# High and low parts of the weights of a transformer step: two tiles against one interleaved tile

## The chip, the cores and the metric

One core of one Trainium2 chip runs the whole program in one launch. The metric is the device time of one execution in microseconds (us); lower is better.

## The reference, cut to what matters

A sequence of 256 tokens with 1,024 channels goes through two blocks. The first has a feed-forward block, a mixer ("pool") and a second feed-forward block, each behind a norm that is modulated by nine vectors made from a condition `c`. The second has two attention mixers ("window" and "causal") and a last norm.

```python
def swiglu(n, w_gate, w_up, w_down):
    return (jax.nn.silu(n @ w_gate) * (n @ w_up)) @ w_down     # 1024 x 2816, 1024 x 2816, 2816 x 1024

mod = (jax.nn.silu(c) @ w_ada[l] + b_ada[l])[:, None, :]
h = h + 0.5 * gt1 * swiglu(modulate(rmsnorm(h, g_ffn1[l]), sh1, sc1), ...)
h = h + gt2 * hybrid_mixer(modulate(rmsnorm(h, g_mix[l]), sh2, sc2), ...)
h = h + 0.5 * gt3 * swiglu(modulate(rmsnorm(h, g_ffn2[l]), sh3, sc3), ...)
...
for i in range(2):                      # window attention, then block attention with all past blocks
    q, k, v, z = split_proj(rmsnorm_2(h, norm_g[i]), w_in, n_kv)
    o = attention(q, k, v).reshape(B, S, MIX_WIDTH) * jax.nn.silu(z)
    h = h + o @ w_out[i]
```

Everything is float32. The products with weight matrices are nearly all of the work.

## The kernel before

The weights stream in as 105 units of 1 MB: 128 partitions of 2,048 elements (`UNIT`). A gate, up or input unit is 8 chunks of 128 rows by 256 columns; a down unit is 2 chunks by 1,024 columns. There are three slots (`NS`), and unit `u` uses slot `u % 3`. SyncE loads a unit into `raw` as soon as the low part of the unit three before it has been made.

A float32 product is made of three passes in the type float32r. ScalarE writes the rounded high part of a unit (`high`, L620, `whi<-raw`), VectorE the rest (`low`, L948, `wlo<-raw,whi`; `low_half` L956 does it in two halves at the end of the pool mixer). The activations are split in the same way (`nhi`/`nlo`, `hhi`/`hlo`, `yhi`/`ylo`). TensorE then forms three matmuls into one accumulator for each 128 x 128 tile of weights and 256 tokens (`split_product`, L1416 to L1418):

```python
mm(to, stat_hi, mov_hi, ...)     # L1416
mm(to, stat_hi, mov_lo, ...)     # L1417
mm(to, stat_lo, mov_hi, ...)     # L1418
```

In each of them the weights are the stationary operand: a weights load (LDWEIGHTS, shown on PEld) reads 128 elements of each partition, and the matmul then streams 256 moving columns. A unit is 16 tiles, so 48 loads and 48 matmuls. The two feed-forward blocks have 33 units each, 1,584 matmuls; the mixers have 39 units. `project` does gate, up and input units; `project_two` two units at once at the start of a block; `down` (in `ffn`) the down units, and `out_product` the output matrices of the first two mixers.

In three places the weights move and the activations stand still: `project_rows` (L1522 to L1524) for the value units V and half of the unit KV, and `out_rows` (L1721 to L1723) for the four output units of the last mixer, with 512 moving columns.

The order of all work is written out by hand: each engine runs its own program, a loop of 9 turns for most of a feed-forward block and a list of steps (`mixer_plan`) for the mixers. In the built program every partition has `whi` at byte 41,088, `wlo` at 65,664, `nhi` at 123,200 and `nlo` at 131,392; `hhi`, `hlo`, `yhi` and `ylo` start, like `nhi`, at 320 modulo 1,024, and the weight tiles at 128 modulo 512. A load walks 512 bytes of a partition, a matmul with 256 moving columns 1,024.

The tile names in the profile are out<-moving,stationary: `sc<-nhi,wlo` is a matmul into bank `sc` with moving `nhi` and stationary `wlo`.

Of the kernel before, what the change touches and what calls it, by code (L numbers as in the profile page):

```python
# [24 lines left out]
P = 128  # L25
# [138 lines left out]

BY_ROWS = range(28, 36)

CHAINED = range(8, 28)
# [33 lines left out]
def build(nc, x, c, w_ada, b_ada, g_ffn1, w1_gate, w1_up, w1_down, g_mix, w_in, w_pool, pool_scale, w_out,  # L203
          g_ffn2, w2_gate, w2_up, w2_down, g_final, norm_g_2, w_in_a_2, sinks_a_2, w_in_b_2, w_out_2,
          final_g_2, shape_consts, out):
    with ExitStack() as ctx:
        def sb(name, shape, dt=F32):
            return ctx.enter_context(nc.sbuf_tensor(name, shape, dt))
# [3 lines left out]


        raw = sb("raw", [P, NS, UNIT])
        whi = sb("whi", [P, NS, UNIT], F32R)
        wlo = sb("wlo", [P, NS, UNIT], F32R)
        ada = sb("ada", [P, 2, DC, UC])
        macc = sb("macc", [P, 2, UC])
        hT = sb("hT", [P, DC, S])
# [177 lines left out]
        block = ctx.enter_context(nc.Block())  # L397


        def rows8(t, s):  # L400
            return t[:, s, :].rearrange("p (c n) -> p c n", c=DC)

        def rows2(t, s):
            return t[:, s, :].rearrange("p (c n) -> p c n", c=2)

        def by_chunk(w):
            return w.rearrange("(c p) n -> p c n", p=P)
# [205 lines left out]
        def _(act):  # L613
            def high(u, reps=None, by=None):

                if u >= UNITS:
                    return
                n = 16 * (u // NS + 1)
                act.wait_ge(landed[u % NS], n + 16 * reps if reps is not None else n)
                nc.scalar.activation(whi[:, u % NS], raw[:, u % NS], ACT.Copy).then_inc(hi_done, 1)  # L620

            def squares(k, chunks=range(DC)):
                for m in chunks:
# [310 lines left out]
        def _(dve):  # L934
# [8 lines left out]
            def low(u, reps=None):  # L943

                if u >= UNITS:
                    return
                dve.wait_ge(hi_done, u + 1 + (3 * reps if reps is not None else 0))
                nc.vector.tensor_tensor(wlo[:, u % NS], raw[:, u % NS], whi[:, u % NS].bitcast(F32),  # L948
                                        ALU.subtract).then_inc(lo_done, 1)

            def low_half(u, i):

                if i == 0:
                    dve.wait_ge(hi_done, u + 1)
                at = slice(i * UNIT // 2, (i + 1) * UNIT // 2)
                ins = nc.vector.tensor_tensor(wlo[:, u % NS, at], raw[:, u % NS, at], whi[:, u % NS, at].bitcast(F32),  # L956
                                              ALU.subtract)
                if i:
                    ins.then_inc(lo_done, 1)

# [450 lines left out]
        def _(pe):  # L1411
# [75 lines left out]
                pe.wait_ge(macc_done, q + 1)  # L1487
                select_sums(q, start_ps[q])

            def project(bank, slot, k=None, chunks=(0, 1), over=range(DC)):  # L1490

                hi, lo = rows8(whi, slot), rows8(wlo, slot)
                order = [(m, ch) for m in chunks for ch in range(DC)]
                if k is not None:
                    order = [(m, ch) for ch in over for m in chunks]
                for m, ch in order:
                    if k is not None and m == 0:
                        pe.wait_ge(nlo_done, DC * tnum[k] + ch + 1)
                    at = slice(m * P, (m + 1) * P)

                    ins = split_product(bank[:, m * S:(m + 1) * S], hi[:, ch, at], lo[:, ch, at],
                                        nhi[:, ch], nlo[:, ch], ch == 0 and (k is None or m == 0), ch == DC - 1)
                return ins

            def project_two(banks, slots, k, signals):

                for step in range(DC + 2):
                    for n, ch in ((0, step), (1, step - 2)):
                        if 0 <= ch < DC:
                            ins = project(banks[n], slots[n], k, over=range(ch, ch + 1))  # L1510
                            if ch == DC - 1:
                                ins.then_inc(signals, 1)

            def project_rows(bank, slot, col, width, at0):

                hi, lo = rows8(whi, slot), rows8(wlo, slot)
                for b in range(2):
                    for ch in range(DC):
                        tok = slice(b * P, (b + 1) * P)
                        to = bank[:, at0 + b * width:at0 + (b + 1) * width]  # L1520
                        w = slice(col, col + width)
                        mm(to, nhi[:, ch, tok], hi[:, ch, w], start=(ch == 0), stop=False, skip_group_check=True)  # L1522
                        mm(to, nhi[:, ch, tok], lo[:, ch, w], start=False, stop=False, skip_group_check=True)
                        ins = mm(to, nlo[:, ch, tok], hi[:, ch, w], start=False, stop=(ch == DC - 1),  # L1524
                                 skip_group_check=True)
                return ins

            def job(st):
# [23 lines left out]
                if kind == "U":  # L1552
                    if st["i"] == 0:
                        pe.wait_ge(lo_done, u + 2)
                        project_two((acc[p % 2], acc[(p + 1) % 2]), (u % NS, (u + 1) % NS), MIX_NORM["pool"], job_done)
                    return
                pe.wait_ge(lo_done, u + 1)
                k = MIX_NORM[st["mixer"]] if st["first"] else None
# [2 lines left out]
                if kind == "V":  # L1561
                    if st["rcol"]:
                        token_columns(MIX_NORM[st["mixer"]])
                    ins = project_rows(bank, u % NS, 0, UC, 0)
                elif kind == "KV":
                    project(bank, u % NS, k, chunks=(0,))
                    ins = project_rows(bank, u % NS, P, P, S)
                elif st["rcol"]:
                    project(bank, u % NS, chunks=(0,))
                    token_columns(MIX_NORM[st["mixer"]])  # L1570
                    ins = project(bank, u % NS, chunks=(1,))
                elif kind == "Q" and st["next"]["kind"] == "TPV":
                    project(bank, u % NS, chunks=(0,))
                    if st["mixer"] == "pool":
                        pe.wait_ge(mod_done, 32)
                    transposes(st["next"], 0)
                    transposes(st["next"], 1)
                    ins = project(bank, u % NS, chunks=(1,))
                elif kind == "Z":
                    project(bank, u % NS, chunks=(0,))  # L1580
                    scores(st["next"], (0, 1))
                    ins = project(bank, u % NS, chunks=(1,))
                else:
                    ins = project(bank, u % NS, k)
                ins.then_inc(job_done, 1)
                if st["first"] and st["mixer"] != "pool":
                    sum_squares(STAT[k], None, True, True)
# [111 lines left out]

            def out_product(st, j, m, chunks, first, last):  # L1700

                hi, lo = rows8(whi, st["u"] % NS), rows8(wlo, st["u"] % NS)
                at = slice(m * P, (m + 1) * P)
                for ch in chunks:
                    if j == 0 and m == 0:
                        y_ready(st, ch)
                    to = out_acc[RESIDUAL[MIX_NORM[st["mixer"]] + 1]][j]
                    ins = split_product(to[:, m * S:(m + 1) * S], hi[:, ch, at], lo[:, ch, at], yhi[:, ch],
                                        ylo[:, ch], first and ch == chunks[0], last and ch == chunks[-1])
                return ins  # L1710

            def out_rows(u, j, chunks):

                tok = slice(j % 2 * P, (j % 2 + 1) * P)
                to = out_acc["last"][j][:, :]
                for ch in chunks:
                    if j == 0:
                        y_ready(PLANS["causal"][-1], ch)
                    slot, i = (u + ch // 4) % NS, ch % 4
                    hi, lo = [t[:, slot, :].rearrange("p (c n) -> p c n", c=4)[:, i] for t in (whi, wlo)]  # L1720
                    mm(to, yhi[:, ch, tok], hi, start=False, stop=False, skip_group_check=True)  # L1721
                    mm(to, yhi[:, ch, tok], lo, start=False, stop=False, skip_group_check=True)  # L1722
                    ins = mm(to, ylo[:, ch, tok], hi, start=False, stop=ch == DC - 1, skip_group_check=True)  # L1723
                return ins
# [99 lines left out]
            def ffn(f):  # L1824
                base, n0, k = FFN_UNIT[f], FB * f, FFN_NORM[f]

                def gate(u, i, reps=None, norm=None):
                    add = reps if reps is not None else 0
                    pe.wait_ge(lo_done, u + 1 + 3 * add)
                    if n0 + i > 0:  # L1830
                        pe.wait_ge(silu_done, n0 + i + add)
                    project(sc[0], u % NS, norm).then_inc(ffn_used, 1)

                def up(u, i, reps=None):
                    add = reps if reps is not None else 0
                    pe.wait_ge(lo_done, u + 1 + 3 * add)
                    if n0 + i > 0:
                        pe.wait_ge(hid_done, n0 + i + add)
                    project(sc[1], u % NS).then_inc(ffn_used, 1)

                def down(u, i, reps=None, buf=0):
                    add = reps if reps is not None else 0
                    hi, lo = rows2(whi, u % NS), rows2(wlo, u % NS)
                    first = reps is None and i == 0
                    pe.wait_ge(lo_done, u + 1 + 3 * add)
                    pe.wait_ge(hlo_done, n0 + i + 1 + add)
# [11 lines left out]
                else:  # L1858
                    pe.wait_ge(lo_done, base + 2)
                    pe.wait_ge(silu_done, n0)  # L1860
                    pe.wait_ge(hid_done, n0)
                    project_two(sc, (base % NS, (base + 1) % NS), k, ffn_used)
                gate(base + 2, 1)
                up(base + 3, 1)
                for m, ins in down(base + 4, 0):
# [110 lines left out]
```

## Time and profile before

| what | us |
|---|---|
| median of 3 executions (lowest, highest) | 743.36 (743.33, 750.12) |
| the profiled execution | 743.8 |
| its span, first to last instruction | 742.0 |
| TensorE matmul busy in it | 710.3 |

The profile is one execution. Starts are counted from the span's start. PE is TensorE's matmuls, PEld its weights loads, DVE VectorE, ACT ScalarE, POOL GpSimd. Matmuls overlap one another, so the distance between two starts, not the length of one, says how fast TensorE goes; a stretch's length divided by the number of matmuls in it gives the same.

### The profile page before, as it was taken

The numbers are of one execution on the slowest core, as the hardware profiler recorded it, in microseconds if no ns is written. First come the engines' busy times: TensorE is split into PE (matmuls) and PEld (weight loads), VectorE is DVE, ScalarE is ACT, GpSimd is POOL, SyncE is SP. The second block draws the span as 40 slices with busy tenths as digits, with TensorE's granted clock in tenths as the row PEclk, the third lists the DMA queues.
The fourth block names the chain that finished last, engine by engine and source line by source line (L and its number), as shares of the span: only waits on it lengthen the run. The fifth ranks groups of instructions, "written<-read, shape, count | busy, mean of one in ns | idle before, by whom it ended". The sixth has DMA issues, their size and how long they took to land.

```text
span 742.0 us, 14116 instructions
## 1 busy us (share of the span) xinstructions
PE 710.3 (96%) x5888; PEld 661.4 (89%) x5888; DVE 489.8 (66%) x738; ACT 367.1 (49%) x559; POOL 77.1 (10%) x73
## 2 busy tenths in 40 slices
PE   5599999999999999989999999999999999999997
PEld 4299999999998988869999999999888889888875
DVE  2469789877866446566445544555989986787853
ACT  4154344343454346546343334336676666746652
POOL 0000066000010680000000000000600002000000
PEclk9589999999998999999999999999999999999999
DMA  9999999998956753275556556555333344554301
GB/s 337 382 362 303 331 372 325 350 327 319 345 180 226 269 193 110 84 229 164 178 179 203 183 174 200 191 170 170 114 115 115 116 147 135 170 163 123 114 1 57
DMA packets 102100, 152.59 MB, mean 206 GB/s; under 512 B 2600, under 2 KB 84268, under 8 KB 101932
## 3 DMA queue, kind: packets, MB, share of 16 engines
q1 hardware_dynamic: 101828, 151.75, 60.2%
q8 instruction: 28, 0.46, 0.3%
q10 hardware_dynamic: 232, 0.28, 0.1%
q14 instruction: 12, 0.10, 0.0%
HBM read 150.97 MB, written 1.05 MB: 205 GB/s over the span
## 4 chain that ended last, share of the span: by engine, by line
PE 42%; DVE 8%; ACT 5%; issue 1%; ACTq 0%; DVEq 0%
PE sc L1416 6%; PE sc L1417 6%; PE sc L1418 6%; PE acc L1416 5%; PE acc L1417 5%; PE acc L1418 5%; DVE wlo L948 3%; ACT whi L620 2%; PE acc L1721 1%; PE acc L1723 1%; PE acc L1722 1%; ACT nhi L649 1%; PE sc L1609 1%; DVE vp L1134 1%; ACT vp L747 1%
## 5 line engine op out<-in xcount | busy, mean ns | idle before, releaser
L948 DVE TENSOR_TENSOR wlo<-raw,whi 128x2048 fp32r<-128x2048 f32 x104 | 241.2, 2321 | 114.8 <-ACT whi L620 114.6
L620 ACT ACTIVATE whi<-raw 128x2048 fp32r<-128x2048 f32 x105 | 200.1, 1908 | 67.5 <-PE sc L1418 59.6
L1416 PE MATMUL sc<-nhi,whi 128*128 128x256 f32 x704 | 197.7, 281 | 2.0 <-DVE nlo L1386 1.6
L1417 PE MATMUL sc<-nlo,whi 128*128 128x256 f32 x704 | 197.2, 280 | 0.0
L1418 PE MATMUL sc<-nhi,wlo 128*128 128x256 f32 x704 | 197.2, 280 | 0.0
L1416 PEld LDWEIGHTS sc<-nhi,whi 128*128 128x128 f32 x704 | 134.9, 192 | 2.5 <-issue 2.5
L1417 PEld LDWEIGHTS sc<-nlo,whi 128*128 128x128 f32 x704 | 133.4, 190 | 0.0
L1418 PEld LDWEIGHTS sc<-nhi,wlo 128*128 128x128 f32 x704 | 133.3, 189 | 0.0
L1416 PE MATMUL acc<-nhi,whi 128*128 128x256 f32 x376 | 109.4, 291 | 2.9 <-DVE wlo L948 1.7
L1417 PE MATMUL acc<-nlo,whi 128*128 128x256 f32 x376 | 104.5, 278 | 0.0
L1418 PE MATMUL acc<-nhi,wlo 128*128 128x256 f32 x376 | 104.4, 278 | 0.0
L1417 PE MATMUL acc<-hlo,whi 128*128 128x256 f32 x320 | 89.1, 279 | 0.0
L1416 PE MATMUL acc<-hhi,whi 128*128 128x256 f32 x320 | 89.1, 279 | 0.0
L1418 PE MATMUL acc<-hhi,wlo 128*128 128x256 f32 x320 | 89.1, 279 | 0.0
L1416 PEld LDWEIGHTS acc<-nhi,whi 128*128 128x128 f32 x376 | 70.8, 188 | 12.0 <-issue 7.6
L1417 PEld LDWEIGHTS acc<-nlo,whi 128*128 128x128 f32 x376 | 70.9, 189 | 0.5 <-issue 0.5
L1418 PEld LDWEIGHTS acc<-nhi,wlo 128*128 128x128 f32 x376 | 70.8, 188 | 0.0
L1416 PEld LDWEIGHTS acc<-hhi,whi 128*128 128x128 f32 x320 | 60.8, 190 | 0.0
L1417 PEld LDWEIGHTS acc<-hlo,whi 128*128 128x128 f32 x320 | 60.1, 188 | 0.0
L1418 PEld LDWEIGHTS acc<-hhi,wlo 128*128 128x128 f32 x320 | 60.1, 188 | 0.0
L1416 PE MATMUL acc<-yhi,whi 128*128 128x256 f32 x160 | 46.8, 292 | 2.0 <-DVE hT L972 1.4
L555 POOL TENSOR_TENSOR std<-sq 128x256 f32<-128x256 f32 x4 | 2.9, 736 | 411.4 <-DVE nlo L1005 200.9
(248 smaller groups left out, 1084.7 us busy)
## 6 DMA issues: line engine op xcount, KB each, us to landing
ada<-in_w_ada_dram SPq DMA_DIRECT2D x23, 1024.0 KB, 7.6
raw<-in_w_gate_dram SPq DMA_DIRECT2D x22, 1024.0 KB, 5.4
raw<-in_w_up_dram SPq DMA_DIRECT2D x22, 1024.0 KB, 5.9
raw<-in_w_down_dram SPq DMA_DIRECT2D x22, 1024.0 KB, 4.9
raw<-in_w_out_dram SPq DMA_DIRECT2D x12, 1024.0 KB, 5.0
raw<-in_w_in_b_dram SPq DMA_DIRECT2D x10, 1024.0 KB, 5.2
xo<-in_w_ada_dram SPq DMA_DIRECT2D x9, 1024.0 KB, 7.5
raw<-in_w_in_a_dram SPq DMA_DIRECT2D x9, 1024.0 KB, 5.2
```

The lines of the kernel that those rows point to most:

```text
L620: nc.scalar.activation(whi[:, u % NS], raw[:, u % NS], ACT.Copy).then_inc(hi_done, 1)
L649: nc.scalar.activation(nhi[:, m], hT[:, m], ACT.Copy, scale=input_gain(k, m)).then_inc(nhi_done, 1)
L747: ins = nc.scalar.activation(prob[:, s, lo:up], prob[:, s, lo:up], ACT.Exp, scale=-1.0, bias=nm[:, s, b:b + 1], accum_out=den[:, s, b:b + 1])
L948: nc.vector.tensor_tensor(wlo[:, u % NS], raw[:, u % NS], whi[:, u % NS].bitcast(F32), ALU.subtract).then_inc(lo_done, 1)
L1134: ins = nc.vector.tensor_tensor_reduce(out=prob[:, s, lo:up], in0=sc[h % 2][:, lo:up], in1=mask[:, lo:up], scale=-1.0, scalar=largest, op0 ...
L1416: mm(to, stat_hi, mov_hi, start=first, stop=False, skip_group_check=True)
L1417: mm(to, stat_hi, mov_lo, start=False, stop=False, skip_group_check=True)
L1418: return mm(to, stat_lo, mov_hi, start=False, stop=last, skip_group_check=True)
L1609: mm(rot_ps[:, :], rotation, src[:, :, :].rearrange("p b n -> p (b n)"), start=True, stop=True).then_inc(rot_done, 1)
L1721: mm(to, yhi[:, ch, tok], hi, start=False, stop=False, skip_group_check=True)
L1722: mm(to, yhi[:, ch, tok], lo, start=False, stop=False, skip_group_check=True)
L1723: ins = mm(to, ylo[:, ch, tok], hi, start=False, stop=ch == DC - 1, skip_group_check=True)
```

## The change

`whi` and `wlo` (two tiles of 3 x 2,048) become one tile `wpair` of 3 x 4,096 at the same place, and everything else keeps its address. In 97 of the 105 units element n of the high part lies at place 2n and element n of the low part at 2n + 1. There ScalarE writes with a step of 8 bytes, VectorE reads the high part and writes the low part with a step of 8 bytes, and a weights load reads 128 elements with a step of 8 bytes, 1,024 bytes from first to last, starting at 128 or 132 modulo 1,024. The 8 units in `APART` (three V, one KV, the last four output units) keep both halves apart, each contiguous. No instruction is added, removed or moved on any engine; `parts` and `rows` replace `rows8` and `rows2`, and functions take the unit's number instead of its slot.

```diff
+APART = [st["u"] for steps in PLANS.values() for st in steps if st["kind"] in ("V", "KV")]
+APART += range(UNITS - 4, UNITS)
...
-        whi = sb("whi", [P, NS, UNIT], F32R)
-        wlo = sb("wlo", [P, NS, UNIT], F32R)
+        wpair = sb("wpair", [P, NS, 2 * UNIT], F32R)
...
-        def rows8(t, s):
-            return t[:, s, :].rearrange("p (c n) -> p c n", c=DC)
-
-        def rows2(t, s):
-            return t[:, s, :].rearrange("p (c n) -> p c n", c=2)
+        def parts(u):
+            both = wpair[:, u % NS, :]
+            if u in APART:
+                return both[:, 0:UNIT], both[:, UNIT:2 * UNIT]
+            return [both.rearrange("p (n t) -> p n t", t=2)[:, :, t] for t in range(2)]
+
+        def rows(u, chunks):
+            return [t.rearrange("p (c n) -> p c n", c=chunks) for t in parts(u)]
...
-                nc.scalar.activation(whi[:, u % NS], raw[:, u % NS], ACT.Copy).then_inc(hi_done, 1)
+                nc.scalar.activation(parts(u)[0], raw[:, u % NS], ACT.Copy).then_inc(hi_done, 1)
...
-                nc.vector.tensor_tensor(wlo[:, u % NS], raw[:, u % NS], whi[:, u % NS].bitcast(F32),
-                                        ALU.subtract).then_inc(lo_done, 1)
+                hi, lo = parts(u)
+                nc.vector.tensor_tensor(lo, raw[:, u % NS], hi.bitcast(F32), ALU.subtract).then_inc(lo_done, 1)
...
-            def project(bank, slot, k=None, chunks=(0, 1), over=range(DC)):
-
-                hi, lo = rows8(whi, slot), rows8(wlo, slot)
+            def project(bank, u, k=None, chunks=(0, 1), over=range(DC)):
+
+                hi, lo = rows(u, DC)
...
-                hi, lo = rows8(whi, st["u"] % NS), rows8(wlo, st["u"] % NS)
+                hi, lo = rows(st["u"], DC)
...
-                    slot, i = (u + ch // 4) % NS, ch % 4
-                    hi, lo = [t[:, slot, :].rearrange("p (c n) -> p c n", c=4)[:, i] for t in (whi, wlo)]
+                    hi, lo = [t[:, ch % 4] for t in rows(u + ch // 4, 4)]
...
-                    hi, lo = rows2(whi, u % NS), rows2(wlo, u % NS)
+                    hi, lo = rows(u, 2)
```

## Rows read from the trace of the kernel before

**Rows 1.** Page: busy time by engine; busy tenths of 40 slices.

```profile
span 742.0 us, 14116 instructions
...
PE 710.3 (96%) x5888; PEld 661.4 (89%) x5888; DVE 489.8 (66%) x738; ACT 367.1 (49%) x559; POOL 77.1 (10%) x73
...
PE   5599999999999999989999999999999999999997
...
PEclk9589999999998999999999999999999999999999
```

**Rows 2.** Waits of TensorE, longest first.

```profile
PE sc L1902 <- DMA kd<-in_b_ada_dram: 7.7, 1, 7.7
...
PE acc L1416 <- DVE wlo L948: 1.7, 1, 1.7
```

**Rows 3.** Windows: half-clock start, both feed-forward blocks, the last two mixers.

```profile
core 0: us, PE busy (x) PEld busy (x) DVE busy (x) ACT busy (x) POOL busy (x), PEclk, DMA share, GB/s
37.08:42.28 5.20, 5.20 (x26) 5.20 (x26) 3.93 (x7) 5.20 (x7) 0.00 (x0) 0.50 1.06 395
42.85:213.42 170.57, 170.57 (x1507) 170.57 (x1506) 138.18 (x95) 70.61 (x53) 24.57 (x12) 1.00 0.95 336
332.85:512.11 179.26, 179.26 (x1523) 179.26 (x1523) 91.43 (x63) 75.82 (x60) 0.00 (x0) 1.00 0.57 183
521.00:707.00 186.00, 181.19 (x1473) 159.72 (x1474) 153.76 (x356) 121.77 (x270) 15.79 (x19) 1.00 0.41 131
```

**Rows 4.** Timeline (start, length), first feed-forward block: two starts three matmuls apart.

```profile
...
149.95 0.28 PE L1416 MATMUL sc<-nhi,whi 128*128 128x256 f32 x1
...
150.29 0.28 PE L1416 MATMUL sc<-nhi,whi 128*128 128x256 f32 x1
...
```

**Rows 5.** Timeline, second feed-forward block: three matmuls apart.

```profile
...
399.87 0.28 PE L1416 MATMUL sc<-nhi,whi 128*128 128x256 f32 x1
...
400.22 0.28 PE L1416 MATMUL sc<-nhi,whi 128*128 128x256 f32 x1
...
```

**Rows 6.** Line L1416, 60 to 200 us: durations min/median/max ns.

```profile
L1416 PE MATMUL acc<-hhi,whi x144: 276/276/276, 61.2 to 196.9; 128*128 128x256 f32 x144
L1416 PEld LDWEIGHTS acc<-hhi,whi x144: 187/188/188, 61.1 to 196.8; 128*128 128x128 f32 x144
```

**Rows 7.** Line L1416, 345 to 505 us.

```profile
L1416 PE MATMUL acc<-hhi,whi x144: 281/281/282, 353.9 to 494.9; 128*128 128x256 f32 x144
L1416 PEld LDWEIGHTS acc<-hhi,whi x144: 192/192/192, 353.8 to 494.8; 128*128 128x128 f32 x144
```

**Rows 8.** Timeline at half clock: three matmuls apart.

```profile
...
40.07 0.41 PE L1416 MATMUL sc<-nhi,whi 128*128 128x256 f32 x1
...
40.71 0.41 PE L1416 MATMUL sc<-nhi,whi 128*128 128x256 f32 x1
...
```

**Rows 9.** Timeline, matmuls with 128 moving columns: first and last of 18.

```profile
...
527.77 0.27 PE L1522 MATMUL acc<-whi,nhi 128*128 128x128 f32 x1
...
529.66 0.28 PE L1524 MATMUL acc<-whi,nlo 128*128 128x128 f32 x1
...
```

**Rows 10.** Groups of matmuls, 215 to 331 us.

```profile
L1418 PE MATMUL acc<-nhi,wlo 128*128 128x256 f32 x96 | 26.8, 279 | 0.0
...
L1418 PE MATMUL acc<-yhi,wlo 128*128 128x256 f32 x80 | 22.3, 279 | 0.0
```

**Rows 11.** Groups of matmuls, 513 to 722 us.

```profile
L1418 PE MATMUL acc<-nhi,wlo 128*128 128x256 f32 x280 | 77.6, 277 | 0.0
...
L1417 PE MATMUL acc<-ylo,whi 128*128 128x256 f32 x80 | 22.3, 279 | 0.0
```

**Rows 12.** Line L948 on VectorE, 43 to 213 us, and L620 on ScalarE, whole span.

```profile
L948 DVE TENSOR_TENSOR wlo<-raw,whi x32: 2278/2293/3095, 42.8 to 211.6; 128x2048 fp32r<-128x2048 f32 x32
...
L620 ACT ACTIVATE whi<-raw x105: 1888/1907/1924, 20.1 to 721.7; 128x2048 fp32r<-128x2048 f32 x105
```

**Rows 13.** Page: the chain that ended last, by engine and line.

```profile
PE sc L1416 6%; PE sc L1417 6%; PE sc L1418 6%; PE acc L1416 5%; PE acc L1417 5%; PE acc L1418 5%; DVE wlo L948 3%; ACT whi L620 2%; PE acc L1721 1%; PE acc L1723 1%; PE acc L1722 1%; ACT nhi L649 1%; PE sc L1609 1%; DVE vp L1134 1%; ACT vp L747 1%
```

More of the change, by code:

```diff
@@ L955, in low_half @@
                 at = slice(i * UNIT // 2, (i + 1) * UNIT // 2)
-                ins = nc.vector.tensor_tensor(wlo[:, u % NS, at], raw[:, u % NS, at], whi[:, u % NS, at].bitcast(F32),
-                                              ALU.subtract)
+                hi, lo = parts(u)
+                ins = nc.vector.tensor_tensor(lo[:, at], raw[:, u % NS, at], hi[:, at].bitcast(F32), ALU.subtract)
                 if i:
@@ L1503, in project, with project_two @@
                 return ins
-            def project_two(banks, slots, k, signals):
+            def project_two(banks, units, k, signals):
                 for step in range(DC + 2):
@@ L1509, in project_two, with project_rows @@
                         if 0 <= ch < DC:
-                            ins = project(banks[n], slots[n], k, over=range(ch, ch + 1))
+                            ins = project(banks[n], units[n], k, over=range(ch, ch + 1))
                             if ch == DC - 1:
                                 ins.then_inc(signals, 1)
-            def project_rows(bank, slot, col, width, at0):
-                hi, lo = rows8(whi, slot), rows8(wlo, slot)
+            def project_rows(bank, u, col, width, at0):
+                hi, lo = rows(u, DC)
                 for b in range(2):
@@ L1554, in job @@
                         pe.wait_ge(lo_done, u + 2)
-                        project_two((acc[p % 2], acc[(p + 1) % 2]), (u % NS, (u + 1) % NS), MIX_NORM["pool"], job_done)
+                        project_two((acc[p % 2], acc[(p + 1) % 2]), (u, u + 1), MIX_NORM["pool"], job_done)
                     return
@@ L1563, in job @@
                         token_columns(MIX_NORM[st["mixer"]])
-                    ins = project_rows(bank, u % NS, 0, UC, 0)
+                    ins = project_rows(bank, u, 0, UC, 0)
                 elif kind == "KV":
-                    project(bank, u % NS, k, chunks=(0,))
-                    ins = project_rows(bank, u % NS, P, P, S)
+                    project(bank, u, k, chunks=(0,))
+                    ins = project_rows(bank, u, P, P, S)
                 elif st["rcol"]:
-                    project(bank, u % NS, chunks=(0,))
+                    project(bank, u, chunks=(0,))
                     token_columns(MIX_NORM[st["mixer"]])
-                    ins = project(bank, u % NS, chunks=(1,))
+                    ins = project(bank, u, chunks=(1,))
                 elif kind == "Q" and st["next"]["kind"] == "TPV":
-                    project(bank, u % NS, chunks=(0,))
+                    project(bank, u, chunks=(0,))
                     if st["mixer"] == "pool":
@@ L1577, in job @@
                     transposes(st["next"], 1)
-                    ins = project(bank, u % NS, chunks=(1,))
+                    ins = project(bank, u, chunks=(1,))
                 elif kind == "Z":
-                    project(bank, u % NS, chunks=(0,))
+                    project(bank, u, chunks=(0,))
                     scores(st["next"], (0, 1))
-                    ins = project(bank, u % NS, chunks=(1,))
+                    ins = project(bank, u, chunks=(1,))
                 else:
-                    ins = project(bank, u % NS, k)
+                    ins = project(bank, u, k)
                 ins.then_inc(job_done, 1)
@@ L1831, in gate @@
                         pe.wait_ge(silu_done, n0 + i + add)
-                    project(sc[0], u % NS, norm).then_inc(ffn_used, 1)
+                    project(sc[0], u, norm).then_inc(ffn_used, 1)
                 def up(u, i, reps=None):
@@ L1838, in up @@
                         pe.wait_ge(hid_done, n0 + i + add)
-                    project(sc[1], u % NS).then_inc(ffn_used, 1)
+                    project(sc[1], u).then_inc(ffn_used, 1)
                 def down(u, i, reps=None, buf=0):
                     add = reps if reps is not None else 0
-                    hi, lo = rows2(whi, u % NS), rows2(wlo, u % NS)
+                    hi, lo = rows(u, 2)
                     first = reps is None and i == 0
@@ L1861, in ffn @@
                     pe.wait_ge(hid_done, n0)
-                    project_two(sc, (base % NS, (base + 1) % NS), k, ffn_used)
+                    project_two(sc, (base, base + 1), k, ffn_used)
                 gate(base + 2, 1)
```

## The prediction

> **What bounds the kernel now.** I read the page's first parts, then TensorE's waits, then windows and timelines of its long stretches. TensorE is busy in 710.3 of 742.0 us, at full clock in nearly every slice after the start [rows 1]. Its waits are small: the longest is 7.7 us at the start, the longest for a weight's low part 1.7 us [rows 2]. So the time is TensorE's own pace, 5,040 matmuls on weights (105 units of 48) and some 850 others.
>
> That pace is not one number. In the first feed-forward block 1,507 matmuls fill 170.57 us, 113.2 ns each; in the second 1,523 fill 179.26 us, 117.7 ns each [rows 3]. The timelines agree: three matmuls take 0.34 us in the one and 0.35 in the other [rows 4, 5]. Code, shapes, slots and addresses are the same, the granted clock is 1.00 in both, no wait stands in either, and the faster block has more traffic beside it (DMA share 0.95 against 0.57, VectorE 138 us against 91). I call the two paces the short step and the long step. They differ in one thing: in the long step the load of line L1416 takes 192 ns where it took 188, and a matmul 281 where it took 276 [rows 6, 7]. A block begins in one step and stays in it to its end.
>
> Two more rows set the floor. At half clock (0.50) a step is 0.64 us / 3 = 213 ns [rows 3, 8], so at full clock the same columns alone would need 107 ns, and the short step is 6 ns above that. With only 128 moving columns 17 steps take 1.89 us, 111 ns each [rows 9]: there the contiguous load, not the streaming, sets the step. So loads come within 2 ns of the short step, and anything that lengthens them by more shows in the total.
>
> The Trainium skill ("TensorE: Matmul & The Clock Gate", "LDWEIGHTS (loading the stationary operand)") gives a load as columns / 1.2 GHz whatever it reads; for 128 that is an estimate of 107 ns, and the 111 ns of [rows 9] agree. By it the load would be as long after the change as before, and the layout could act only by how load and streaming meet.
>
> **The change part by part.** No instruction comes, goes or moves. What changes is the step of addresses in 97 units.
>
> *TensorE.* Before, a load walks 512 bytes while the matmul beside it walks 1,024; afterwards both walk 1,024, so their distance in memory stays the same through a step, whichever tile it is. The long step looks like the two streams meeting: it appears with nothing else changed, is kept up by the rhythm of hi, hi, lo, and lengthens one load of the three. If equal walks remove the meeting, every step becomes the short one. I take 113.2 ns from the first block and count against the profiled execution:
> - second block: 1,584 x (117.7 - 113.2) = 7.1 us;
> - last down unit of the first block, 48 matmuls at 279 ns where the block had 276 (within [rows 10]): 0.2 us;
> - mixers: their 1,488 changed matmuls are at mean lengths of 277 to 279 ns against 276 [rows 10, 11]. Per line, 96 x 3 + 64 x 3 (the 80 less 16 of that down unit) early and 280 x 1 + 64 x 3 late, times three lines, is 2.9 us. TensorE is busy in 181 of 186 us there [rows 3], but VectorE and ScalarE also stand in the chain, so I let two thirds count: 1.9 us.
>
> Together 9.2 us. The profiled execution took 743.8 us (its span 742.0 and 1.8 around it), 0.4 above the median of 743.36, so I subtract there: 743.8 - 9.2 = 734.6 us.
>
> No row shows a load with a step of 8 bytes. From below it is bounded by the contiguous load, 111 ns [rows 9]; from above by the slowest pace of a step in the trace, 213 ns [rows 8]. I take the contiguous value, to which every full-clock row is near, and keep the rest for the range.
>
> *ScalarE and VectorE.* A high part is 1,907 ns and a low part 2,293 ns in the median [rows 12]. No row has a step of 8 bytes on a tile of this size either. From below I bound it at no change, as the element count, engine and type stay; from above at twice the length. I take no change. Cover: in the first feed-forward block VectorE is idle for 170.6 - 138.2 = 32.4 us, and holds 32 low parts there [rows 3, 12]; each could grow by 1.0 us, 44%, before VectorE sets the pace. In the mixers there is less: `wlo` is 3% and `whi` 2% of the chain [rows 13], 37 us, so a tenth more costs up to 3.7 us.
>
> The rule that speaks to this is the Trainium skill's on lines of 16 bytes ("Advanced Engine Details and Errata", "Memory Cachelines"): full rate needs at least two accesses in each line. A step of 8 bytes leaves exactly two fp32, so by the rule loads, reads and writes cost what they did and the sum stands; but nothing is to spare, and where two hits fall short the fourth rival holds. No row of this trace has such a step, so the rule is neither borne out nor refuted here.
>
> *SyncE, DMA, waits.* A unit is loaded when the low part three units before is done; unchanged. In the first block a step shorter than 113 ns would ask for more than the 336 GB/s of [rows 3]; the start shows 395, so there is room for the 2% of the first rival.
>
> **The rivals.**
> 1. *The short step shrinks too.* If its 6 ns above 107 also come from meeting, both blocks fall to the load's 111 ns: 1,536 x 2.0 = 3.1, 1,584 x 6.5 = 10.3, the last down unit 0.3, mixers 1,488 x 4.0 x 2/3 = 4.0 us, 17.7 in all: 726 us. For it: half clock shows no loss over the streaming. Against it: the 6 ns stay the same over 1,507 matmuls, whatever else runs; they look like the moving operand's own.
> 2. *Nothing changes.* If the step is chosen by where TensorE stood when a block began, the layout has no say: 743.4 us. For it: the same addresses gave both steps. Against it: one load in three is longer in the long step, so loads take part. Were load and streaming balanced at a step between the two, the first block's loss and the second's gain would cancel, and it would come to the same.
> 3. *The long step everywhere.* If equal walks make load and streaming meet always, the first block pays 1,536 x 4.5 = 6.9 us and the mixers 1,488 x 4.5 less the 2.9 they have, two thirds of it, 2.5: 753 us.
> 4. *The load becomes the bound* (slower). A load now passes through twice as many bytes. If it meets the streaming twice as often, the long step's extra doubles to 9 ns everywhere: 1,536 x 9 = 13.8, 1,584 x 4.5 = 7.1, mixers (1,488 x 9 - 2.9 us) x 2/3 = 7.0, so 772 us. Place: every load of the 97 units; it decides as soon as a load passes 113 ns, 2 above [rows 9]. At the upper bound of 213 ns it would be 3,168 x 98 ns = 310 us in the blocks and about 97 in the mixers, some 1,150 us. For it: the margin is only 2 ns. Against it: most of a load's 188 ns is already beside a matmul, and the long step prolongs one in three by only 4.
> 5. *Slower engines.* Twice 2,293 ns would put 73 us more on VectorE in the first block, 41 over its idle time, and up to 37 in the mixers: about 820 us.
>
> **How the numbers follow.** Forecast, short step everywhere: 0.36. Rival 1: 0.10, rival 2: 0.22, rival 3: 0.11, rival 4: 0.14, rival 5: 0.07. Faster by over 1%, which is about what a measurement here can tell from no change, means below 735.9 us. My 734.6 is barely under it: with mixers that give nothing it would be 736.5, with all of theirs 733.6; and 731 to 739 is its own range. So I give three quarters of it, 0.28, to faster and 0.08 to the same: faster 0.28 + 0.10 = 0.38; same 0.08 + 0.22 = 0.30; slower 0.11 + 0.14 + 0.07 = 0.32. The range 724 to 774 holds the forecast, rivals 1 to 3 and rival 4 at 772; what lies outside is rival 5 and the larger prices of rival 4, some 0.15.
>
> **What would show it.** Right: windows over both blocks that give 113 ns a matmul, matmuls of 276 ns and loads of 188 on all three lines; high and low parts still near 1,907 and 2,293 ns. Rival 1 shows as 111 ns; rival 2 as one block still at 118; rivals 3 and 4 as 118 or more in both, and loads longer than 192; rival 5 as longer lines of the high and low parts and waits of TensorE for them. Wrong altogether would be a gain with the two steps still there.

## The result and the profile after

| what | before | after |
|---|---|---|
| median of 4 executions, us | 743.35 (735.19 to 750.12) | 762.23 (760.35 to 762.67) |
| ratio after / before | | 1.031, interval 1.026 to 1.037 |
| the profiled execution, us | 743.8 | 761.96 |
| its span, us | 742.0 | 760.1 |

The change makes the kernel slower by 3%. The ratio compares fast executions alone (slow ones lie over 1.5% above the fastest of their kernel); the quotient of the two medians is 1.025. The profiled execution before is one whose second block ran in the long step; the 18.1 us that follow are counted against it. The page of the kernel after, in the parts that answer to [rows 1], and its two groups of the units' high and low parts (busy us, mean ns | idle before):

```profile
span 760.1 us, 14116 instructions
...
PE 729.5 (96%) x5888; PEld 682.3 (90%) x5888; DVE 490.6 (65%) x738; ACT 386.1 (51%) x559; POOL 74.1 (10%) x73
...
PEclk9899999999998999999999999999999999999999
...
L956 DVE TENSOR_TENSOR wpair<-raw,wpair 128x2048 fp32r<-128x2048 f32 x104 | 241.0, 2320 | 129.8 <-ACT wpair L627 128.8
L627 ACT ACTIVATE wpair<-raw 128x2048 fp32r<-128x2048 f32 x105 | 219.1, 2090 | 67.0 <-PE sc L1425 60.1
```

The same instructions, the clock granted as before, and TensorE busy 19.2 us longer (729.5 against 710.3) in a span that is 18.1 longer. ScalarE is also 19.0 us busier, VectorE hardly. TensorE's waits show that it is not kept waiting for them; they answer to [rows 2] and are as short as there:

```profile
PE sc L1908 <- DMA kd<-in_b_ada_dram: 7.3, 1, 7.3
...
PE acc L1423 <- DVE wpair L956: 1.6, 1, 1.6
```

So it is TensorE's own pace again. The windows inside both feed-forward blocks and over the last two mixers, against [rows 3]:

```profile
core 0: us, PE busy (x) PEld busy (x) DVE busy (x) ACT busy (x) POOL busy (x), PEclk, DMA share, GB/s
42.00:222.00 180.00, 180.00 (x1502) 180.00 (x1502) 137.77 (x94) 76.76 (x53) 20.87 (x12) 1.00 0.90 320
340.00:520.00 180.00, 180.00 (x1507) 178.85 (x1500) 91.19 (x67) 81.44 (x62) 0.00 (x0) 1.00 0.56 185
530.00:716.00 186.00, 182.23 (x1446) 162.79 (x1446) 152.94 (x351) 124.63 (x269) 18.04 (x21) 1.00 0.39 127
```

A fixed window counts matmuls cut at both its edges, up to three too many, so the step is read better from starts in the timeline. In the first block, three matmuls apart (start, length), to be held against [rows 4, 5]:

```profile
149.96 0.28 PE L1423 MATMUL acc<-hhi,wpair 128*128 128x256 f32 x1
...
150.32 0.28 PE L1423 MATMUL acc<-hhi,wpair 128*128 128x256 f32 x1
```

0.36 us for three: 120 ns, where the short step was 113 and the long one 118. Counted from start to start over 160 us of the second block it is 120.0 ns as well. Line L1423 is L1416 of before, here from 60 to 200 us (against [rows 6]) and from 345 to 505 us (against [rows 7]):

```profile
L1423 PEld LDWEIGHTS acc<-hhi,wpair x131: 194/194/194, 60.9 to 199.9; 128*128 128x128 f32 x131
L1423 PE MATMUL acc<-hhi,wpair x131: 282/283/283, 61.0 to 200.0; 128*128 128x256 f32 x131
...
L1423 PEld LDWEIGHTS acc<-hhi,wpair x133: 193/193/193, 365.0 to 504.7; 128*128 128x128 f32 x133
L1423 PE MATMUL acc<-hhi,wpair x133: 283/283/283, 365.1 to 504.8; 128*128 128x256 f32 x133
```

On this line loads take 193 to 194 ns and matmuls 283 in both blocks; the two paces of before have become one, slower than either. All three lines now have loads of 193 to 195 ns, where the long step of before lengthened the load of L1416 alone. ScalarE and VectorE write with gaps too, but it is not their writes that hold up the loads: in the first window above they are busy for 43% and 77% of the time, and the loads of L1423 there, 194 ns at the least and at the most, don't vary with it.

At half clock, though, nothing has changed. Two starts there, 21 matmuls apart, give 4.48 / 21 = 213 ns, as in [rows 8]:

```profile
36.08 0.41 PE L1425 MATMUL sc<-nhi,wpair 128*128 128x256 f32 x1
...
40.56 0.41 PE L1425 MATMUL sc<-nhi,wpair 128*128 128x256 f32 x1
```

Where the 18.1 us come from, worked out from the starts of the first and last matmuls on weights of each stage:

| stage, us | before | after | difference |
|---|---|---|---|
| start | 36.7 | 35.5 | -1.2 |
| first feed-forward block | 176.7 | 186.7 | +10.0 |
| from it through the first mixer | 117.7 | 119.7 | +2.0 |
| second feed-forward block | 181.0 | 184.3 | +3.3 |
| last two mixers | 229.9 | 233.9 | +4.0 |

Both blocks lose about what a step of 120.0 ns asks for: 1,536 x (120.0 - 113.2) = 10.4 us and 1,584 x (120.0 - 117.7) = 3.6 us.

### The profile page after: what moved, and what is told of

Read it like the earlier page. It is cut to its first block, busy times and chain, and to the rows that moved or that the text cites. A ratio compares the mean times of both kernels' runs of the same rounds, so it can differ in the third digit from the quotient of the medians.

```text
span 760.1 us, 14116 instructions
## 1 busy us (share of the span) xinstructions
PE 729.5 (96%) x5888; PEld 682.3 (90%) x5888; DVE 490.6 (65%) x738; ACT 386.1 (51%) x559; POOL 74.1 (10%) x73
## 4 chain that ended last, share of the span: by engine, by line
PE 45%; DVE 6%; ACT 4%; issue 1%; DVEq 0%; ACTq 0%
PE acc L1423 7%; PE acc L1425 6%; PE acc L1424 6%; PE sc L1423 6%; PE sc L1425 6%; PE sc L1424 5%; DVE wpair L956 2%; ACT wpair L627 1%; PE acc L1727 1%; PE acc L1729 1%; PE acc L1728 1%; PE sc L1616 1%; PE sc L1632 1%; PE sc L1633 1%; ACT nhi L656 1%; PE tp L1476 1%
## 5 line engine op out<-in xcount | busy, mean ns | idle before, releaser
L956 DVE TENSOR_TENSOR wpair<-raw,wpair 128x2048 fp32r<-128x2048 f32 x104 | 241.0, 2320 | 129.8 <-ACT wpair L627 128.8
L627 ACT ACTIVATE wpair<-raw 128x2048 fp32r<-128x2048 f32 x105 | 219.1, 2090 | 67.0 <-PE sc L1425 60.1
L1423 PE MATMUL sc<-nhi,wpair 128*128 128x256 f32 x704 | 200.5, 285 | 1.6 <-DVE nlo L1393 1.6
L1424 PE MATMUL sc<-nlo,wpair 128*128 128x256 f32 x704 | 199.3, 283 | 0.0
L1425 PE MATMUL sc<-nhi,wpair 128*128 128x256 f32 x704 | 199.1, 283 | 0.0
L1423 PEld LDWEIGHTS sc<-nhi,wpair 128*128 128x128 f32 x704 | 137.4, 195 | 2.1 <-issue 2.1
L1425 PEld LDWEIGHTS sc<-nhi,wpair 128*128 128x128 f32 x704 | 138.0, 196 | 0.0
L1424 PEld LDWEIGHTS sc<-nlo,wpair 128*128 128x128 f32 x704 | 137.8, 196 | 0.0
L1423 PE MATMUL acc<-nhi,wpair 128*128 128x256 f32 x376 | 111.2, 296 | 2.8 <-DVE wpair L956 1.6
L1425 PE MATMUL acc<-nhi,wpair 128*128 128x256 f32 x376 | 106.0, 282 | 0.0
L1423 PE MATMUL acc<-hhi,wpair 128*128 128x256 f32 x320 | 90.5, 283 | 0.0
L1425 PE MATMUL acc<-hhi,wpair 128*128 128x256 f32 x320 | 90.0, 281 | 0.0
L1423 PEld LDWEIGHTS acc<-nhi,wpair 128*128 128x128 f32 x376 | 73.2, 195 | 11.9 <-issue 8.1
L1425 PEld LDWEIGHTS acc<-nhi,wpair 128*128 128x128 f32 x376 | 73.1, 194 | 0.0
L1425 PEld LDWEIGHTS acc<-hhi,wpair 128*128 128x128 f32 x320 | 62.2, 194 | 0.0
L1423 PEld LDWEIGHTS acc<-hhi,wpair 128*128 128x128 f32 x320 | 61.9, 194 | 0.0
L1423 PE MATMUL acc<-yhi,wpair 128*128 128x256 f32 x160 | 47.5, 297 | 1.8 <-DVE hT L979 1.4
```

The lines of the kernel that those rows point to most:

```text
L627: nc.scalar.activation(parts(u)[0], raw[:, u % NS], ACT.Copy).then_inc(hi_done, 1)
L956: nc.vector.tensor_tensor(lo, raw[:, u % NS], hi.bitcast(F32), ALU.subtract).then_inc(lo_done, 1)
L1423: mm(to, stat_hi, mov_hi, start=first, stop=False, skip_group_check=True)
L1424: mm(to, stat_hi, mov_lo, start=False, stop=False, skip_group_check=True)
L1425: return mm(to, stat_lo, mov_hi, start=False, stop=last, skip_group_check=True)
```

## The experiments

Each time was taken on one chip beside executions of the kernel before. The dispute: does the *load* set the step because its operand has gaps (theory L), or do load and streaming *meet* in memory (theory M)?

**1. and 2. Half as many moving columns for each load.** Each matmul of 256 columns becomes two of 128, each with its own load, once in the kernel after and once in the kernel before. The streaming gets short, so a load shows by itself.

```diff
-                mm(to, stat_hi, mov_hi, start=first, stop=False, skip_group_check=True)
...
+                for n, (w, x) in enumerate(((stat_hi, mov_hi), (stat_hi, mov_lo), (stat_lo, mov_hi))):
+                    for h in range(2):
+                        half = slice(h * P, (h + 1) * P)
+                        ins = mm(to[:, half], w, x[:, half], start=first and n == 0 and h == 0, stop=last and n == 2,
```

> The kernel after, but each matmul on 256 columns is two on 128 columns, each with its own weights load (twice the loads, the same result). Theory L (the interleaved load takes longer by itself and sets the step): with only 128 moving columns streaming beside it the load still sets the step, so it stays near 120 ns, and about 9,400 steps of 120 ns give some 1,300 us. Theory M (the load is not longer; load and streaming meet where both walk 1,024 bytes): the 128 columns walk only 512 bytes, the meeting is gone and the step is what the contiguous load gives, 109 to 111 ns.

> The kernel before with the same split into 128 columns: contiguous loads. Both theories expect the step of the contiguous load, 109 to 111 ns, as in the 18 matmuls of the unit KV. Theory L expects it about 10 ns below the same split of the kernel after; theory M expects both alike.

Measured 1,907.4 us (interleaved) and 1,890.2 (contiguous). Both totals missed: most of the execution ran at half clock. Windows of TensorE, first of the interleaved kernel, then of the contiguous one: 100 us of the first block, and a stretch near the end, the output units of the window mixer and the input units behind them, 336 matmuls long, in which the full clock was granted:

```profile
core 0: us, PE busy (x), PEclk, DMA share, GB/s
100.00:200.00 100.00, 100.00 (x471) 0.50 0.24 84
1712.15:1751.61 39.46, 39.46 (x336) 1.00 0.26 85
```

```profile
100.00:200.00 100.00, 100.00 (x470) 0.50 0.24 84
1702.28:1739.69 37.41, 37.41 (x336) 1.00 0.26 86
```

At full clock the same 336 take 39.46 us against 37.41. From start to start, 334 steps take 39.34 us against 37.30: 117.8 ns against 111.7. In that stretch a load takes 196 ns interleaved and 192 contiguous:

```profile
L1426 PEld LDWEIGHTS acc<-yhi,wpair 128*128 128x128 f32 x160 | 22.1, 196 | 0.2 <-issue 0.2
```

```profile
L1419 PEld LDWEIGHTS acc<-yhi,whi 128*128 128x128 f32 x80 | 12.2, 192 | 0.2 <-issue 0.2
```

With half the streaming the interleaved step falls only from 120 to 118 ns: the load sets it, with 128 columns beside it as with 256. The contiguous one comes within 1 ns of the 111 of [rows 9]. The 6 ns between the layouts are still there when the streaming is short, which is what L says (it expected about 10); under M they should have gone with it. At half clock both layouts need 213 ns for each matmul, so the time of an interleaved load does not double with the halved clock, which would make it 236 ns: what the gaps cost stays hidden under a step that is slower anyway.

**3. Another distance between weights and activations.** In the kernel after, 832 bytes of padding behind `wpair` move the activations from 320 to 128 modulo 1,024, where the weights start.

```diff
         wpair = sb("wpair", [P, NS, 2 * UNIT], F32R)
+        sb("pad", [P, 208])
```

> The kernel after with 832 unused bytes behind the weight tile, so that activations start at 128 modulo 1,024 like the weights and no longer 192 bytes further on. Theory L: no change, 120 ns a step and 762 us. Theory M: the distance between the two walks is what matters, so the step moves away from 120, either to 113 (about 735 us) or well above 120.

763.1 us, and the window of the first block, columns as in the windows above, holds as many matmuls, to one, as the kernel after, where the same 100 us hold 836:

```profile
100.00:200.00 100.00, 100.00 (x835) 100.00 (x835) 79.45 (x53) 42.11 (x29) 20.85 (x12) 1.00 0.87 311
```

Where the two streams lie to each other has no say at the two distances tried. With experiments 1 and 2, M, on which my forecast rested, does not explain the 120 ns.

**4. A step of 16 bytes.** Two tiles of 128 elements of the high part and two of the low part are woven element by element, so that neighbours of one load are 16 bytes apart.

```diff
-            return [both.rearrange("p (n t) -> p n t", t=2)[:, :, t] for t in range(2)]
...
+            return wpair[:, u % NS, :].rearrange("p (b j t q) -> p b q j t", t=2, q=2, j=P)[:, :, :, :, t]
```

> The kernel after with four elements woven instead of two (high and low of two neighbouring weight tiles), so that a load reads 128 elements with a step of 16 bytes and walks 2,048. Theory L: the load grows with the stretch that it walks; if by as much again as from 4 to 8 bytes (about 10 ns above the contiguous 111) the step is 130 ns and the time about 800 us, if each element now costs a fetch of its own up to 213 ns and 1,150 us. Theory M: the two walks are unequal again, and the step falls back to 113 to 118 ns, 735 to 750 us.

1,287.6 us. The window of the first block, a line of loads in it, and the page's groups of low and high parts:

```profile
100.00:200.00 100.00, 100.00 (x427) 100.00 (x426) 52.29 (x28) 38.67 (x15) 18.30 (x12) 1.00 0.47 169
```

```profile
L1440 PEld LDWEIGHTS sc<-nhi,wpair x94: 332/332/332, 100.2 to 199.8; 128*128 128x128 f32 x94
```

```profile
L972 DVE TENSOR_TENSOR wpair<-raw,wpair 128x2048 fp32r<-128x2048 f32 x104 | 395.4, 3805 | 326.9 <-ACT wpair L643 326.8
L643 ACT ACTIVATE wpair<-raw 128x2048 fp32r<-128x2048 f32 x105 | 396.3, 3780 | 166.9 <-PE sc L1442 129.8
```

From start to start these matmuls are 235.5 ns apart, nearly twice the 120 of the kernel after, at full clock and with loads of 332 ns. Twice the bytes walked, twice the step. The step and the time are above the highest price that L had given (213 ns, 1,150 us), and far from M's 113 to 118 ns. The means of the two groups take in the 8 units of `APART`, which are contiguous; in the first feed-forward block, from 60 to 380 us, a low part takes 3,931 ns and a high part 3,949 in the mean.

**5. One tile, but contiguous loads.** The same woven `wpair`, now in whole tiles of 128 elements: high, high, low, low, each 512 bytes in a piece.

```diff
-            return [both.rearrange("p (n t) -> p n t", t=2)[:, :, t] for t in range(2)]
...
+            return wpair[:, u % NS, :].rearrange("p (b q t j) -> p b q t j", t=2, q=2, j=P)[:, :, :, t, :]
```

> The kernel after with its one tile, but whole tiles of 128 high and 128 low parts take turns in it, so that a load reads 512 bytes without a gap. Theory L (the gap between elements makes the load longer): back to steps of 113 and 118 ns, 735 to 750 us as the kernel before, ScalarE's high part at 1,907 ns. Theory T (sharing one tile, or where the high and low parts lie, costs the time): 120 ns and 762 us stay.

Median 734.0 us against 740.9 of the kernel before, ratio 0.995 (0.990 to 1.000). Windows of both blocks, and the page's group of the high parts:

```profile
100.00:200.00 100.00, 100.00 (x885) 100.00 (x884) 82.65 (x57) 42.12 (x31) 18.77 (x11) 1.00 0.93 333
380.00:480.00 100.00, 100.00 (x885) 100.00 (x884) 51.40 (x31) 40.60 (x30) 0.00 (x0) 1.00 0.58 192
```

```profile
L643 ACT ACTIVATE wpair<-raw 128x2048 fp32r<-128x2048 f32 x105 | 200.2, 1909 | 66.0 <-PE sc L1442 54.6
```

The short step is back in both blocks, and a high part takes 1,909 ns as before. So neither the common tile nor high and low parts that lie close to one another cost anything; the gap between elements does, for TensorE and for ScalarE.

**6. Only the feed-forward units interleaved.** `APART` gets every unit of the mixers.

```diff
-APART = [st["u"] for steps in PLANS.values() for st in steps if st["kind"] in ("V", "KV")]
+APART = [st["u"] for steps in PLANS.values() for st in steps if "u" in st]
```

> The kernel after with only the 66 units of the feed-forward blocks interleaved; all units of the mixers are kept apart. Theory L: 120 ns a step in both blocks, 113 to 118 in the mixers; against the profiled execution before, 10.0 us more in the first block and 3.3 in the second and nothing in the mixers, so 755 to 757 us. If ScalarE's longer high part (2,108 ns against 1,907) is what the mixers pay for, they too come back, with steps as before.

752.6 us, below what was expected. Both blocks keep their 120 ns; the last mixers, in a window as long as that of [rows 3], are back at 1,474 matmuls (1,473 there), where the kernel after has 1,446:

```profile
100.00:200.00 100.00, 100.00 (x836) 100.00 (x835) 78.81 (x54) 42.86 (x30) 20.13 (x12) 1.00 0.87 312
380.00:480.00 100.00, 100.00 (x836) 100.00 (x835) 48.22 (x29) 41.91 (x29) 0.00 (x0) 1.00 0.55 182
...
530.00:716.00 186.00, 181.70 (x1474) 160.20 (x1474) 153.70 (x357) 121.78 (x270) 15.68 (x18) 1.00 0.40 131
```

The mixers' part of the loss is thereby their own units': by the stages' starts the last two take 230.0 us, against 229.9 in the kernel before and 233.9 in the one after. The miss, some 3 us, lies in the stretch from the first block's last matmul on weights to the first mixer's first, 20.0 us here and 23.0 in the kernel after; it is 19.9 in experiment 5 and 22.8 in the kernel before, and in experiment 9, with the very kernel of experiment 5, it is 22.9: it varies with no change to the kernel.

**7. A step of 12 bytes.** Three tiles of one part woven, for 15 of 16 loads of a unit; high and low parts stay apart. ScalarE and VectorE each write the woven 15 tiles of a unit and its 16th in two instructions. The cut shows the line that weaves.

```diff
+            return x[:, 0:W3].rearrange("p (b j q) -> p b q j", q=3, j=P)
```

> High and low parts apart; in each, three weight tiles are woven, so that 15 of 16 loads read 128 elements with a step of 12 bytes. If a load costs a fetch for each stretch of 16 bytes that it touches (64 at a step of 8 bytes: 120 ns; 128 at 16 bytes: 235 ns; so 1.85 ns each), 96 fetches are 178 ns a step and the time is near 1,030 us. If it goes by the bytes walked from first to last in a straight line between 1,024 (120) and 2,048 (235), 1,536 bytes are 178 ns as well; if two elements in a stretch are needed for full rate and one is not, the step is a mixture of 120 and 235 in which half of all elements stand alone.

994.0 us, 3% under the 1,030 expected. Timeline in the first block, starts three matmuls apart, and the groups of high and low parts, now of 1,920 elements:

```profile
149.76 0.34 PE L1443 MATMUL acc<-hhi,wpair 128*128 128x256 f32 x1
...
150.29 0.34 PE L1443 MATMUL acc<-hhi,wpair 128*128 128x256 f32 x1
...
150.81 0.34 PE L1443 MATMUL acc<-hhi,wpair 128*128 128x256 f32 x1
```

```profile
L979 DVE TENSOR_TENSOR wpair<-raw,wpair 128x1920 fp32r<-128x1920 f32 x97 | 273.6, 2821 | 209.5 <-ACT wpair L647 209.4
L646 ACT ACTIVATE wpair<-raw 128x1920 fp32r<-128x1920 f32 x97 | 274.1, 2825 | 108.1 <-PE sc L1445 90.9
```

(150.81 - 149.76) / 6 = 175 ns. All three readings of the expectation gave 178, so this does not choose among them; it shows that the cost grows evenly. The three steps with gaps lie close to one line through zero. A load walks 1,024, 1,536 and 2,048 bytes, which is 64, 96 and 128 stretches of 16 bytes: 120 / 64 = 1.88, 175 / 96 = 1.82 and 235.5 / 128 = 1.84 ns each. The contiguous load is not on it: 32 stretches would be 60 ns, and it takes 111. So the runs fit a load that takes the longer of two times, one for its 128 elements (111 ns at full clock) and one for the memory it walks (some 1.85 ns for 16 bytes). Whether what counts is the stretches touched or the bytes walked these runs don't tell apart; pieces of 16 contiguous bytes with gaps between would, and were not tried.

**8. The other order of the three products.** The kernel before with high·high, low·high, high·low: weights high, low, high in place of high, high, low. This asks whether that rhythm keeps up the long step of before, as I had argued.

```diff
-                mm(to, stat_hi, mov_lo, start=False, stop=False, skip_group_check=True)
-                return mm(to, stat_lo, mov_hi, start=False, stop=last, skip_group_check=True)
+                mm(to, stat_lo, mov_hi, start=False, stop=False, skip_group_check=True)
+                return mm(to, stat_hi, mov_lo, start=False, stop=last, skip_group_check=True)
```

> The kernel before, contiguous, with the three matmuls in the order high x high, low x high, high x low, so that no two neighbouring loads read the same weights. Theory R (the rhythm high, high, low keeps the long step up): the long step is gone, 113 ns in both blocks, 735 us in every execution. Theory P (the long step is only a relation of start times): blocks in either step, between 735 and 750 us as before.

Median 740.1 us, ratio 0.997 (0.992 to 1.002), and single executions spread from 731.9 to 749.5 as those of the kernel before do beside it, from 735.3 to 749.9. The order makes no difference that was measured. The one execution that was profiled has the short step in both blocks (885 matmuls in 100 us of each), so the totals alone speak here; experiment 10 shows the long step itself with this order.

**9. and 10. Experiment 5 again, and with that order.**

> The kernel with whole tiles of high and low parts taking turns, a second time and with more executions. Theory V (this placement makes the long step rarer): most executions near 733 to 736 us again, median 1% below the kernel before. Theory C (the first ten executions fell in the short step by chance): the same spread as the kernel before, 733 to 749 us, median near 741.

> The same placement with the matmuls in the order high x high, low x high, high x low. If placement and order both bear on how often the long step comes up, nearly all executions lie near 733; if neither does, they spread between 733 and 749 us like the kernel before.

736.6 us with a ratio of 0.998 (0.994 to 1.002), and 739.5 with 1.000 (0.996 to 1.005). The small gain of experiment 5 did not come again; as the intervals of 5 and 9 overlap, half a per cent is neither shown nor excluded. In the profiled execution of 9 the second block has the long step, with the same code that had the short one in experiment 5:

```profile
100.00:200.00 100.00, 100.00 (x885) 100.00 (x884) 82.63 (x56) 41.33 (x31) 17.96 (x10) 1.00 0.93 333
380.00:480.00 100.00, 100.00 (x852) 100.00 (x851) 47.78 (x31) 40.52 (x30) 0.00 (x0) 1.00 0.58 188
```

The same in experiment 10, where the order of the products is high, low, high:

```profile
380.00:480.00 100.00, 100.00 (x852) 100.00 (x851) 48.29 (x30) 40.06 (x30) 0.00 (x0) 1.00 0.57 184
```

So the rhythm high, high, low is not what keeps up the long step (theory R of experiment 8 falls). The profiled executions of 5, 8 and 9 took 733.6, 736.4 and 742.2 us: the first two have the short step in both blocks and differ by the stretch of 20 or 23 us named in experiment 6, the third has the longer stretch and the long step. No version was shown to beat the kernel before.

## Why the prediction was wrong

- **What bounds the kernel** was right: TensorE's pace, not a wait, and a pace that differs by block. So was the warning that loads come within 2 ns of the short step, so that anything that lengthens them shows in the total.
- **The step that failed** is "I take the contiguous value, to which every full-clock row is near". No row had a load with gaps, so nearness to the rows said nothing about it. Between bounds of 111 and 213 ns I took the end at which nothing happens, beside a margin of 2 ns; the load measures 118 ns with half the streaming (experiment 1) and 120 beside 256 columns (experiment 3), and the step is that load, as rival 4 has it, which "decides as soon as a load passes 113 ns". I gave that rival 0.14.
- **Equal walks remove the meeting**: no run shows such a meeting. Another distance (experiment 3) changed nothing, and the long step came with another order of the products too (experiment 10); but in the kernel after the load hides whatever a meeting would add, so it is not shown that there was none. The terms of the sum that rested on it, -7.1, -0.2 and -1.9 us, became +3.3 in the second block, and +2.0 and +4.0 in the stretches with the mixers. The first block, counted at no change, lost 10.0.
- **Rival 4 had the right bound, its price was too high.** That the load becomes the bound, because it passes through twice the bytes, is what the runs show. Its price came from the meeting of load and streaming, twice as often, which no run shows, so that it came near is partly luck. It put the step 9 ns above the short one; measured are 6.8. With that its own sum gives 10.4 + 3.6 + (1,488 x 6.8 ns - 2.9 us) x 2/3 = 4.8, together 18.8 us for the 18.1 found. The mixers gave 6.0 us where this says 4.8. The chain that ended last holds five of ScalarE's high parts in the last two mixers, each 0.2 us longer than those in the chain before; whether the difference is theirs was not separated.
- **ScalarE and VectorE**: VectorE as forecast, 2,294 ns in the median against 2,293 [rows 12]. ScalarE not: 2,108 against 1,907, a tenth more. In the blocks it costs nothing there, as TensorE's waits above show. The medians of high and low parts in the kernel after:

```profile
L627 ACT ACTIVATE wpair<-raw x105: 1892/2108/2141, 19.8 to 739.8; 128x2048 fp32r<-128x2048 f32 x105
```

```profile
L956 DVE TENSOR_TENSOR wpair<-raw,wpair x104: 2277/2294/3104, 24.9 to 741.7; 128x2048 fp32r<-128x2048 f32 x104
```

- **The rules of the Trainium skill.** The rule on lines of 16 bytes ("Advanced Engine Details and Errata", "Memory Cachelines") asks for at least two accesses in each line for the full rate. With the two that a step of 8 bytes leaves, it held for VectorE, but not for ScalarE (2,108 ns against 1,907) nor for the loads (118 to 120 ns against 111), so here the measurements decide. With one access in a line ScalarE takes 3,949 ns, VectorE 3,931 and a load 235.5, which agrees with the penalty that it names. The rule that a load takes its columns / 1.2 GHz ("TensorE: Matmul & The Clock Gate", "LDWEIGHTS (loading the stationary operand)") holds here for contiguous operands at full clock, 111 ns where it gives 107, and not for steps of 8, 12 and 16 bytes.
- **The range** held the time only because it reached to rival 4, whose price was too high; the forecast itself had the wrong sign.
- **A count**: the prediction has 5,040 matmuls on weights; the trace has 4,968, as the last four output units take half as many matmuls and the unit KV more. The sum uses 1,488 of the mixers' matmuls, which is right, and nothing else hangs on it.

What stays open is what decides whether a contiguous block runs in the short or the long step. It is not the distance alone, since the same addresses gave both, nor the order of the products; both steps occur with one tile as with two. In the five traces with contiguous loads and 256 columns (the kernel before and experiments 5, 8, 9 and 10) the first block has the short step each time, and the second the long one in three.

## What to carry to other kernels

Keep the stationary operand contiguous along its columns. At full clock a weights load of 128 float32r columns cost the longer of about 111 ns and 1.85 ns for each 16 bytes that it walked, so even a step of two elements put it past a matmul of 256 columns that follows every 113 ns; bring data side by side in whole tiles instead, as in experiment 5. And where a profile shows work that stays hidden by a margin of only 2 ns, forecast a loss from any change to that work whose cost no row shows.

## What the runs showed of the hardware that was not expected

- With 128 moving columns for each load, TensorE was busy without a gap and yet was granted 0.50 of the clock (1.2 GHz) for most of the execution, in both layouts (0.63 in the mean over the span), where the same blocks in matmuls of 256 columns had 1.00. So 128 columns took 213 ns, where 256 had taken 113.
- An interleaved load does not take twice as long at half the clock: at 0.50 interleaved and contiguous loads both give steps of 213 ns, where twice 118 would be 236.
- The engines differ in what gaps cost them. With 8 bytes VectorE loses nothing and ScalarE a tenth; with 12 bytes they take 1.47 ns an element each (2,821 and 2,825 for 1,920), where contiguous elements take 2,293 / 2,048 = 1.12 and 1,907 / 2,048 = 0.93; with 16 bytes 1.92 and 1.93 (3,931 and 3,949 for 2,048).
